# Upper and lower activations streamed through one 512-column matmul in three feed-forward layers, with GpSimd adding the two halves

## The reference: what is computed

```python
def sq_relu_mlp(h, w_in, w_out):
    a = jax.nn.relu(h @ w_in)
    return (a * a) @ w_out
...
def conv_glu(h, w_up, conv_w, conv_b, w_down):
    gate, val = jnp.split(h @ w_up, 2, axis=-1)
    gate = depthwise_conv(gate, conv_w, conv_b)
    return (jax.nn.silu(gate) * val) @ w_down
```

## Time and profile before

| | |
|---|---|
| median of 3 runs | 1002.38 us (1001.0 to 1002.65) |
| profiled execution, its own time | 1002.42 us |
| its span in the trace | 1000.6 us |
| PE busy | 965.4 us, 96% of the span |
| DVE busy | 682.0 us, 68% |
| ACT busy | 518.0 us, 52% |
| POOL busy | 53.3 us, 5% |
| mean granted TensorE clock | 0.994 of full speed |

### The profile page before, as it was taken

How to read it: one execution, slowest core, us unless ns; L and a number is a source line. 1 busy time by engine, 2 the same in 40 slices (tenths; PEclk the granted TensorE clock), 3 DMA queues, 4 the chain that set the end, 5 groups by cost and what they waited for, 6 DMA issues and landing times. The chain is left out here.

```text
span 1000.6 us, 14873 instructions
## 1 busy us (share of the span) xinstructions
PE 965.4 (96%) x5844; PEld 828.2 (83%) x5844; DVE 682.0 (68%) x948; ACT 518.0 (52%) x715; POOL 53.3 (5%) x71
## 2 busy tenths in 40 slices
PE   7989999999999999999999999999988989999997
PEld 5468889988978877899999887889866789999996
DVE  2676658999755666647788665467565687777775
ACT  2565665445446665554545554454566454444443
POOL 0310000000001110000001000000011000000000
PEclk9999999999999999999999999999997999999999
DMA  9132666767655732677988562232210535555541
GB/s 355 75 127 84 228 236 226 276 228 275 249 204 195 236 126 93 218 283 287 336 301 328 176 252 76 94 126 85 84 43 10 199 124 222 184 182 179 182 169 43
DMA packets 29520, 185.06 MB, mean 185 GB/s; under 512 B 3616, under 2 KB 4320, under 8 KB 10016
## 3 DMA queue, kind: packets, MB, share of 16 engines
q1 hardware_dynamic: 24192, 155.54, 42.8%
q0 software_dynamic: 4416, 28.31, 7.7%
q10 hardware_dynamic: 864, 0.55, 0.2%
HBM read 181.77 MB, written 2.62 MB: 184 GB/s over the span
## 5 line engine op out<-in xcount | busy, mean ns | idle before, releaser
L2027 DVE TENSOR_TENSOR split<-raw,split 128x2048 fp32r<-128x2048 f32 x122 | 279.6, 2292 | 178.5 <-ACT split L1467 177.0
L1467 ACT ACTIVATE split<-raw 128x2048 fp32r<-128x2048 f32 x121 | 231.5, 1913 | 233.5 <-PE bank L732 219.9
L730 PE MATMUL bank<-acts,split 128*128 128x256 f32 (+1 forms) x960 | 278.1, 290 | 2.7 <-DVE acts L2067 1.4
L731 PE MATMUL bank<-acts,split 128*128 128x256 f32 (+1 forms) x960 | 276.7, 288 | 0.0
L732 PE MATMUL bank<-acts,split 128*128 128x256 f32 (+1 forms) x960 | 276.7, 288 | 0.0
L730 PE MATMUL bank<-split,acts 128*128 128x512 f32 (+1 forms) x544 | 211.6, 389 | 2.7 <-DVE acts L2709 1.3
L731 PE MATMUL bank<-split,acts 128*128 128x512 f32 (+1 forms) x544 | 208.7, 384 | 0.0
L732 PE MATMUL bank<-split,acts 128*128 128x512 f32 (+1 forms) x544 | 208.6, 383 | 0.0
L730 PEld LDWEIGHTS bank<-acts,split 128*128 128x128 f32 x960 | 183.7, 191 | 9.9 <-DVE split L2027 3.3
L731 PEld LDWEIGHTS bank<-acts,split 128*128 128x128 f32 x960 | 183.8, 191 | 3.5
L732 PEld LDWEIGHTS bank<-acts,split 128*128 128x128 f32 x960 | 183.8, 191 | 1.9
(11 more groups left out here) (251 smaller groups left out, 1022.8 us busy)
## 6 DMA issues: line engine op xcount, KB each, us to landing
raw<-w_mlp SPq DMA_DIRECT2D x64, 1024.0 KB, 4.8
raw<-w_glu SPq DMA_DIRECT2D x22, 1024.0 KB, 4.8
bias<-w_ada POOLq DMA_DIRECT2D x14, 1024.0 KB, 6.8
raw<-w_qkv SPq DMA_DIRECT2D x12, 1024.0 KB, 5.5
arena<-w_glu_down SPq DMA_DIRECT2D x22, 512.0 KB, 3.3
work<-w_ada POOLq DMA_DIRECT2D x10, 1024.0 KB, 6.2
raw<-w_mla_o SPq DMA_DIRECT2D x4, 1024.0 KB, 5.1
raw<-w_moba_o SPq DMA_DIRECT2D x4, 1024.0 KB, 4.7
```

The costliest lines, as they stand in the source:

```text
L730: pe.matmul(out_, a[0], b[0], start=first, stop=False)
L731: pe.matmul(out_, a[0], b[1], start=False, stop=False)
L1467: return act.activation(out_, in_, ACT.Copy)
L2027: v.tensor_tensor(split[:, c % 2, 1, 0:n], raw[:, c % 2, 0:n], split[:, c % 2, 0, 0:n].bitcast(F32), ALU.subtract).then_inc(lo_ready, 1)
```

## The change

In all three feed-forwards an up chunk is now two units with one bank each, one per block of 128 features. For each contraction tile, the upper weights are loaded once and stream upper and lower activations together, 512 columns (two blocks of 256 from `acts`), so that one bank holds upper x upper in its first half and upper x lower in its second; the third product, lower x upper, is a 256-column matmul into the first half. A chunk is 16 matmuls of 512 and 16 of 256 columns. The two halves of a bank have to be added: ACT copies the bank to `both_t` in SBUF (`halves_out`, 128 x 512), and POOL adds the halves (`halves_added`, 128 x 256), which it does twice per chunk. What read the bank before now reads the sum in SBUF: relu in the two squared-ReLU layers (its result goes back in place), the taps and the product in the glu.

ACT's copy of the first unit stands ahead of its `used`, that of the second behind it, and ahead of relu or behind the centre tap. In DVE's loop the `beside` job of a chunk now stands ahead of the hidden layer's lower part, but for the last few chunks. POOL's loads of modulation weights stand at fixed places between its additions.

```diff
-GEMMS = [("mla_in", 0, 4, 1), ("mla_uq", 0, 6, 1), ("mla_ukv", 0, 8, 1), ("mla_o", 4, 4, 2), ("mlp0", 32, 16, 1),
-         ("qkv", 12, 12, 2), ("moba_o", 4, 4, 2), ("mlp1", 32, 16, 1),
+GEMMS = [("mla_in", 0, 4, 1), ("mla_uq", 0, 6, 1), ("mla_ukv", 0, 8, 1), ("mla_o", 4, 4, 2), ("mlp0", 32, 32, 1),
+         ("qkv", 12, 12, 2), ("moba_o", 4, 4, 2), ("mlp1", 32, 32, 1),
...
-         ("out", 4, 4, 2), ("glu", 22, 22, 1)]
+         ("out", 4, 4, 2), ("glu", 22, 44, 1)]
...
+        both_t = view(arena, 9216, 2, 2, T)
...
+        up_t = view(arena, 2560, 2, 2, T)
...
+            def halves_added(name, s, dst):
+
+                for f in range(2):
+                    u = GU[name] + 2 * s + f
+                    gemm_gone(pool, u)
+                    pool.tensor_tensor(dst[:, f, :], both_t[:, f, 0, :], both_t[:, f, 1, :], ALU.add).then_inc(up_summed, 1)
...
+            def mlp(name, layer, first, last, land, after):
+
+                due = {j: ada_done(layer, j - 2) for j in range(first + 2, last)}
+                for s in range(16):
+                    halves_added(name, s, relu_t[:, s % 2, :].rearrange("p (a b) -> p a b", a=2))
...
+                    for j, n in due.items():
+                        if n in (2 * s - 2, 2 * s - 1):
+                            pool.wait_ge(ada_used, j - 1)
+                            ada_load(j, land)
...
+            def wide_products(u, w, n, ks=range(KD)):
+
+                bank = gbank(u + n)
+                for k in ks:
+                    w_hi, w_lo = (p[:, k, n * P:(n + 1) * P] for p in w)
+                    both, hi = acts[:, 0, :, k * T:(k + 1) * T], acts[:, 0, 0, k * T:(k + 1) * T]
+                    if k < KD - 1:
+                        pe.matmul(bank[:, :], w_hi, both, start=k == 0, stop=False)
+                        pe.matmul(bank[:, 0:T], w_lo, hi, start=False, stop=False)
+                    else:
+                        pe.matmul(bank[:, 0:T], w_lo, hi, start=False, stop=False)
+                        pe.matmul(bank[:, :], w_hi, both, start=False, stop=True).then_inc(gemm_ready, 1)
...
                     else:
-                        cols_unit(c0 + n, u0 + s, (0, 1), (0, 0), i)
+                        wide_unit(c0 + n, u0 + 2 * s, i)
...
+            def halves_out(name, s, f, i=None):
+
+                u = GU[name] + 2 * s + f
+                gemm_out(act, u, i, 8)
+                copy(both_t[:, f], gbank(u)[:, :].rearrange("p (a b) -> p a b", a=2)).then_inc(gemm_free[u % 4], 1)
...
                 def hidden(s, i=None):
-                    u = GU[name] + s
-                    act.activation(relu_t[:, s % 2, :], gbank(u)[:, :], ACT.Relu).then_inc(gemm_free[u % 4], 1)
-                    act.wait_ge(gemm_free[u % 4], u // 4 + 1 if i is None else i + (u // 4 + 1))
+                    halves_out(name, s, 1, i)
+                    n = 2 * s + 2 + SUM0[name]
+                    act.wait_ge(up_summed, n if i is None else 8 * i + n)
+                    act.activation(relu_t[:, s % 2, :], relu_t[:, s % 2, :], ACT.Relu).then_inc(rectified, 1)
+                    act.wait_ge(rectified, HID0[name] + s + 1 if i is None else 4 * i + (HID0[name] + s + 1))
...
-                released(act, GC["glu"] + s, i, 4)
-                act.activation(gact[:, b, :], gbank(u)[:, 0:T], ACT.Identity, scale=w, bias=bb).then_inc(glu_mid, 1)
+                halves_out("glu", s, 0, i)
+                act.wait_ge(up_summed, 8 * k + (2 * s + 1 + SUM0["glu"]))
+                act.activation(gact[:, b, :], up_t[:, b, 0, :], ACT.Identity, scale=w, bias=bb).then_inc(glu_mid, 1)
+                halves_out("glu", s, 1, i)
...
                     used(c0 + n)
+                    if n < 2 * steps - 3:
+                        beside(n)
                     if not seq[n][0]:
                         hidden(seq[n][1])
-                    beside(n)
+                    if n >= 2 * steps - 3:
+                        beside(n)
...
-                v.tensor_tensor(prod_t[:, b, :], gbank(u)[:, T:2 * T], gact[:, b, :], ALU.mult)\
-                    .then_inc(gemm_free[u % 4], 1)
+                v.wait_ge(up_summed, 8 * k + (2 * s + 2 + SUM0["glu"]))
+                v.tensor_tensor(prod_t[:, b, :], up_t[:, b, 1, :], gact[:, b, :], ALU.mult).then_inc(glu_prod, 1)
```

More of the change, by code:

```diff
@@ L103, in plan @@
                 if not is_down:
-                    released.append(("gemm", unit + step + 1))
+                    released.append(("gemm", unit + 2 * (step + 1)))
                 elif step < n // 2 - 1:
@@ L165, with ada_done @@
 HID0 = dict(mlp0=0, mlp1=16, glu=32)
+SUM0 = dict(mlp0=0, mlp1=32, glu=64)
+def ada_done(layer, j):
+    return max(n for n, items in ADA[layer].items() if any(x[0] == j for x in items))
 RAW = ("h0", "m0", "h1", "m1")
@@ L660, in _ @@
             roots(3, 7)
-            pool.wait_ge(act_lo, LO0["mlp0"] + 1)
-            for j in range(2):
-                ada_load(j, att)
-            roots(7, 8)
-            for j in range(2, 10):
-                pool.wait_ge(ada_used, j - 1)
-                ada_load(j, att)
+            def mlp(name, layer, first, last, land, after):
+                due = {j: ada_done(layer, j - 2) for j in range(first + 2, last)}
+                for s in range(16):
+                    halves_added(name, s, relu_t[:, s % 2, :].rearrange("p (a b) -> p a b", a=2))
+                    if s == 1:
+                        pool.wait_ge(act_lo, LO0[name] + 1)
+                        for j in range(first, first + 2):
+                            ada_load(j, land)
+                        roots(after[0], after[0] + 1)
+                    for j, n in due.items():
+                        if n in (2 * s - 2, 2 * s - 1):
+                            pool.wait_ge(ada_used, j - 1)
+                            ada_load(j, land)
+                    if s == 11:
+                        roots(*after[1])
+            mlp("mlp0", 0, 0, 10, att, (7, (8, 8)))
             for m in range(2):
@@ L691, in _ @@
             roots(10, 11)
-            pool.wait_ge(act_lo, LO0["mlp1"] + 1)
-            for j in (10, 11):
-                ada_load(j, bias)
-            roots(11, 12)
-            for j in range(12, 24):
-                pool.wait_ge(ada_used, j - 1)
-                ada_load(j, bias)
-            roots(12, 14)
+            mlp("mlp1", 1, 10, 24, bias, (11, (12, 13)))
+            roots(13, 14)
             pool.memset(cumr[:, :].bitcast(F32), 0.0).then_inc(zeros_ready, 1)
@@ L706, in _ @@
                 pool.tensor_tensor(diagonal, diagonal, other, ALU.add).then_inc(w_summed, 1)
-            roots(14, len(ROOTS))
+            roots(14, 16)
+            for s in range(KF2):
+                halves_added("glu", s, up_t[:, s % 2])
+            roots(16, len(ROOTS))
         @block.tensor
@@ L816, in first_up @@
                     for n in range(2):
-                        for k in range(k0, k0 + tiles):
-                            ins = product(gbank(u)[:, n * T:(n + 1) * T], tuple(p[:, k, n * P:(n + 1) * P] for p in w),
-                                          act_pair(0, k, 0, T), n == 0 and k == 0, n == 1 and k == KD - 1)
-                ins.then_inc(gemm_ready, 1)
+                        wide_products(u, w, n, range(k0, k0 + tiles))
             def mlp(name, norm, steps, tiles, turns, after=None, then=None):
@@ L1425, in up @@
                     return
-                cols_unit(GC["glu"] + s, GU["glu"] + s, (0, 1), (0, 0), i)
+                wide_unit(GC["glu"] + s, GU["glu"] + 2 * s, i)
             def down(s, i=None):
@@ L1477, in used @@
             def used(c, i=None, pitch=0):
-                per = {"gemm": 4, "down": pitch // 2}.get(RELEASED[c][0], 0)
+                per = {"gemm": 8 if pitch == 8 else 4, "down": pitch // 2}.get(RELEASED[c][0], 0)
                 released(act, c, i, per)
@@ L2840, in glu @@
             def glu(s, i=None):
[L2842 removed]
+                b, k = s % 2, 0 if i is None else i
                 v.wait_ge(glu_mid, 4 * k + (s + 1))
```

28 lines of the change are left out of this document (18 added, 10 removed).

## The result

The changed kernel takes 1045.82 us (median of 4 runs, 1041.44 to 1048.64) against 1002.32 (1001.0 to 1002.65): **1.0433 times as long, 95% interval 1.0388 to 1.0477**. Slower was right; 1018 us was 28 us too low, and the range (to 1035) too narrow. The profiled execution took 1048.16 us, its span is 1045.3.

The account below looks back on a forecast made before the run. TensorE was taken as the bound, 96% busy, with ACT and DVE close behind. From 1002.4 us, +7.0 for the squared-ReLU layers and +8.3 for the glu, TensorE's gain included, gave 1018 us; range 997 to 1035.

Parts of the forecast that it names:

- TensorE's gain of 0.17 per up chunk: All three feed-forwards: wide matmuls shorten an up chunk from 5.75 to 5.58 us, -9.2 us over 54 chunks.
- The rival of 993 us: Whole kernel: everything beside TensorE is hidden and only its 9.2 us gain is left; chance 0.08.
- POOL waits for DVE's operation to end, then needs 0.58; it wins the boundary; DVE is held 0.5: POOL's additions: excluded by DVE operations with two SBUF inputs, they get in at the next boundary and delay DVE 0.5 us.
- The third rival's 1051 us: POOL loses at the boundaries, waiting for a modulation product in mlp0 and mlp1 and the scaling in the glu; chance 0.12.
- First down chunk 2.3 us late: mlp0 and mlp1: the first down chunk waits for up 0's hidden part; +4.6 us for two layers.
- End of mlp1 +2.5: End of mlp1: the last hidden chunk's lower part comes 2.7 us later with no TensorE work to hide it; +2.5 taken.
- Further pairs +0.13 each: mlp0 and mlp1, each later down and up pair: half of a 0.26 us weight delay is paid, 28 times, +3.6 us.
- Loads of the modulation weights ... I take 0: mlp0 and mlp1: these loads are issued a few us later at no cost; some 4 us if they land late in mlp1.
- the 0.26 of lateness: Squared-ReLU layers: TensorE wants the next split weights at 11.05 us and gets them at 11.31.
- Indicator pairs +0.4 each, bounds 0 and 0.8: mlp0, four pairs with a 2.35 us DVE indicator: half of DVE's 0.8 us excess is paid; +1.7 us in all.
- The glu's start +5.25: Glu start: down 1 comes 25.5 us after up 0 ends instead of 20.25.
- Glu steps 8.70: Glu: ACT and DVE's loop, counted from D (end of ACT's last copy), becomes the bound; 8.70 us a step against 8.50.

Follow-up runs that it names:

- small_loads: Changed kernel with all modulation loads save the first two of each layer bringing 256 of 2048 columns: 1038.9 us, 1.0359 of the kernel before.
- small_indicators: Changed kernel with DVE's indicator operations in mlp0 making 1/16 of their columns, POOL clearing the rest ahead of the layer: 1037.2 us, 1.0386.
- early_copies: Changed kernel with ACT copying both banks ahead of its split in mlp0 and mlp1: 1023.3 us, 1.0228 of the kernel before.
- experiment 6: Two variants of the changed kernel: mlp0's indicators at 1/16 of their columns, 1037.2 us; all columns, cut so no pair has 256, 1042.4 us.
- only_mlps: The change in mlp0 and mlp1 alone, with the glu of the kernel before: 1030.1 us, 1.0296 of the kernel before.
- loads_ahead: Changed kernel with modulation loads due behind a down chunk issued by POOL ahead of the next up unit's addition: 1049.8 us, 1.0481.

## Why the prediction was wrong

- **TensorE's gain of 0.17 per up chunk:** nearly. Chunks take 5.63 us, 0.12 less. The rival of 993 us did not come even without any sum: that kernel takes 998.5.
- **POOL waits for DVE's operation to end, then needs 0.58; it wins the boundary; DVE is held 0.5:** right, by the rows above (0.59; 0.53). The third rival's 1051 us was near the time by luck: in it POOL loses at the boundaries, and here it wins them.
- **First down chunk 2.3 us late:** right. The last up matmul of mlp1's first chunks starts at 438.75 and down 0 at 440.79, 2.04 us in place of 0.12, in mlp0 the same; TensorE in mlp1:

```profile
438.75 0.39 PE L845 MATMUL bank<-acts,split 128*128 128x512 f32 x1
440.79 0.47 PE L754 MATMUL bank<-split,acts 128*128 128x512 f32 x1 [1.64 <-DVE acts L2452]
```

- **End of mlp1 +2.5:** right, 2.7 (26.85 us against 24.14, see the result).
- **Further pairs +0.13 each:** right only where nothing else goes on. The last pair, from 587.04 to 598.23, took 11.19 us (11.22 - 0.17 + 0.13 would be 11.18). But the 11 pairs from 451.96 to 587.04 took 12.28 each, against 11.22 before: 11.7 us. The step that failed is **"Loads of the modulation weights ... I take 0"**. POOL issues them behind its additions, the weight loads start later behind late splits, and the two collide. small_loads gives 7.9 us for it. I had given some 4 as the bound, and for another reason, that DVE would wait for them, and did the sum chunk by chunk as if the 0.26 of lateness were the only thing that a late split starts.
- **Indicator pairs +0.4 each, bounds 0 and 0.8:** mis-sized. Ahead of the up chunk behind them TensorE now waits 2.5 us, in four places, against 0.5 before: 2.0 each, 8 us instead of 1.7. I counted DVE's work for a pair, but not where in the pair it begins. DVE ahead of the first of these stalls (the down chunk starts at 170.18, the next up chunk at 178.06), then the same place before (the down chunk starts at 166.70):

```profile
167.76 2.29 DVE L2081 TENSOR_TENSOR split<-raw,split 128x2048 fp32r<-128x2048 f32 x1 [1.12 <-ACT split L1509]
169.97 1.75 DVE L2468 CUSTOM_DVE_ANT_0 arena<-work,arena 128x1024 f32<-128x1024 f32 x1
...
172.91 2.82 DVE L2218 SCALAR_TENSOR_TENSOR arena<-bias,t5c 128x2048 bf16<-128x2048 f32 x1
175.66 2.28 DVE L2081 TENSOR_TENSOR split<-raw,split 128x2048 fp32r<-128x2048 f32 x1
```

```profile
163.18 2.29 DVE L2027 TENSOR_TENSOR split<-raw,split 128x2048 fp32r<-128x2048 f32 x1 [1.51 <-ACT split L1467]
...
170.06 2.28 DVE L2027 TENSOR_TENSOR split<-raw,split 128x2048 fp32r<-128x2048 f32 x1
```

The row of work begins 2.42 us ahead of the down chunk in place of 3.52, 1.10 later; a product (1.75 for 1.22) and the indicator (2.82 for 2.35) are each held, 1.00 together; and the next `split_lo` stands behind all of it, 2.1 us later. That is the 2.0. small_indicators, in which these stalls are 0.5 us, shows that they need the indicator's length; early_copies, in which they are 1.6 to 1.7, that they need the late start too.

- The term that I had not at all: **the clock**. Two of the up chunks behind these stalls ran at 0.50 for a part and took 7.27 and 7.24 us, the two others 5.70 and 5.75: 3.1 us.
- Missed and small: behind ACT's two table loads of 1.28 us (131.48 and 134.71) the up chunk at 140.96 and the down chunk at 147.67 start 1.2 us after the matmul before them; before, there was one such wait, of 0.85. That the table loads are the cause is argued from their place alone.
- **The glu's start +5.25:** right, 5.65 (down 1 is 31.79 after up 0, it was 26.14). Behind it the clock again: down 1 takes 5.28 us, not 2.75, and from down 1 to down 2 are 10.88 us, not 8.50, +2.4, in no term of mine.
- **Glu steps 8.70:** 8.94 on the mean from down 3 to down 19, +7.0 us in all where I had 3.4. POOL was done 1.85 after D, as I had it (1.84). But ACT starts 0.25 us after POOL's end (932.17 against 931.92; 0.18 in most steps), where I took 0.04, and the centre tap from SBUF takes 0.60, not the silu's 0.40: 0.3 to 0.4 us late from here on, in a loop with no room. The Trainium skill, page SBUF — State Buffer, section Who interferes with whom, gave the exclusion that I built on, and the trace agrees: POOL's addition, ready since 930.63, ends 0.58 us after `down_low` (931.34).

Of the 28 us, by these readings, the modulation loads make about 8, the indicator pairs 6, the clock 5 to 6, the glu's step 4, TensorE's smaller gain 3. These overlap and are not measured apart (experiment 6 says it of the clock); what the runs show is each stretch's loss and what gives it back.

## What to carry to other kernels

A time bound for a single chunk says little when the helper engines have a fixed order and 1.5 us of room: once one hand-off uses up the room, every other thing that was hidden (a load's collision, a long operation, a table load) comes out, and here one of them cost 8 us where I had put nothing. Before you add a step to the busy engines, sum the loop of each of them with its queue in order, loads included, and look for the slack of what stands behind it. If the step must come, place it where the engine that it excludes is waiting anyway: one line moved gave back 2.05 of the 4.33%, some 21 of 43 us.

## What the runs showed of the hardware

- A POOL addition and a DVE operation with two SBUF inputs don't overlap even for 32 columns: it waited 1.5 us and ended 0.11 us after DVE's operation. And the full addition of 256 columns holds DVE in turn, 1.75 us instead of 1.22, the one of 32 columns hardly, 1.27.
- TensorE's granted clock fell to 0.50 in mlp0 behind two waits of 2.5 us (from start to start of two matmuls) of the changed kernel, and not behind two others of the same length. Over changed, only_mlps, small_loads and loads_ahead it fell behind 5 of 13 such waits. In the up and down chunks of all kernels it fell behind none of 2.4 us or less, and at the glu's start behind each of 3.2 to 4.9 us. It stayed low for 3.4 to 6.8 us. What decides it stays open.
- From POOL's end to ACT's start took 0.25 us at the glu's centre tap shown and 0.04 at relu in mlp1 (POOL ended at 529.40, relu began at 529.44). The changed kernel's 32 relus all have 0.03 or 0.04. So have the taps of the six glu steps outside the program's loop; the 16 in the loop have 0.17 to 0.26. Only the tap takes its scale and bias from a place that the loop counter gives. Whether that is the reason was not tried.
